# Adding the gMLP gate bias: from VectorE to sixteen one-row matmuls on TensorE

## The reference, cut to what matters

```python
def even_mixer(h, w_in, gmlp_w, gmlp_b, w_out, n_chunks):
    ...
    vn = (vf - jnp.mean(vf, axis=-1, keepdims=True)) * lax.rsqrt(jnp.var(vf, axis=-1, keepdims=True) + EPS)
    vn = vn.reshape(bsz, n_chunks, CHUNK, B_HEADS, B_DIM)
    z = jnp.einsum('hts,bnshc->bnthc', gmlp_w, vn) + gmlp_b.T[:, :, None]
    yb = u * z.reshape(bsz, t, B_HEADS, B_DIM)
    y = jnp.concatenate([ya.reshape(bsz, t, A_WIDTH), yb.reshape(bsz, t, B_WIDTH)], axis=-1)
    return y @ w_out
```

## Time and profile before

| what | value |
|---|---|
| median of three runs | 1981.9 us |
| the profiled execution's own time | 1978.92 us |
| its span (first to last instruction) | 1977.1 us |
| TensorE (PE) matmul busy | 1804.6 us, 91% |
| TensorE weight loads (PEld) busy | 1327.7 us, 67% |
| VectorE (DVE) busy | 837.1 us, 42% |
| ScalarE (ACT) busy | 660.7 us, 33% |
| chain that ended last, by engine | PE 69%, DMA 13%, DVE 10%, ACT 4%, SP's queue 3% |
| mean granted TensorE clock | 0.956 of full speed |
| time to landing of the broadcast bias load | 7.0 us |

### The profile page before, as it was taken

One profiled execution on the slowest core, in us unless ns is written; L12 is line 12 of the kernel. 1 busy time (PEld: TensorE's weight loads), 2 busy tenths in 40 slices (PEclk: granted clock), 3 DMA queues, 4 the chain that ended last, 5 costly groups with the idle time before them and its releaser, 6 DMA issues.

```text
span 1977.1 us, 28301 instructions
## 1 busy us (share of the span) xinstructions
PE 1804.6 (91%) x11584; PEld 1327.7 (67%) x11584; DVE 837.1 (42%) x1208; ACT 660.7 (33%) x829; POOL 3.4 (0%) x6
## 2 busy tenths in 40 slices
PE   4899899999999888988869999999989889998887
PEld 2667576787787678977857787766636777763433
DVE  2534522333233556467546975554203544420002
ACT  3232322221122355444336764444003434400001
POOL 0000000000000000000000000000000000000000
PEclk8899999999999899998968999999999999999997
DMA  8644166334532222221136989999999999999994
GB/s 320 252 160 149 45 243 226 136 96 141 200 92 80 64 84 66 64 79 40 65 126 216 369 298 363 409 409 409 408 409 404 357 360 380 389 409 409 409 409 167
DMA packets 161843, 479.96 MB, mean 243 GB/s; under 512 B 14976, under 2 KB 58160, under 8 KB 155568
## 3 DMA queue, kind: packets, MB, share of 16 engines
q1 hardware_dynamic: 161712, 478.14, 64.3%
HBM read 477.03 MB, written 1.05 MB: 242 GB/s over the span
## 4 chain that ended last, share of the span: by engine, by line
PE 69%; DMA 13%; DVE 10%; ACT 4%; SPq 3%; issue 2%; DVEq 0%; ACTq 0%
PE ps L603 15%; PE ps L604 14%; PE ps L605 14%; PE ps L1275 5%; DMA arena<-in_moe_up 5%; DMA raw<-in_moe_up 4%; PE ps L1346 3%; DMA arena<-in_moe_w 3%; SPq L553 2%; DVE w_lo L1769 2%; PE ps L617 2%; PE ps L1264 2%; PE ps L636 2%; PE ps L1096 1%; ACT w_hi L1415 1%
## 5 line engine op out<-in xcount | busy, mean ns | idle before, releaser
L1769 DVE TENSOR_TENSOR w_lo<-raw,w_hi 128x1024 fp32r<-128x1024 f32 x242 | 293.1, 1222 | 426.7 <-ACT w_hi L1415 424.2
L1415 ACT ACTIVATE w_hi<-raw 128x1024 fp32r<-128x1024 f32 x242 | 253.1, 1056 | 503.2 <-PE ps L605 399.3
L603 PE MATMUL ps<-h_hi,w_hi 128*128 128x512 f32 (+1 forms) x736 | 286.3, 389 | 27.3 <-DVE h_lo L1813 24.0
L604 PE MATMUL ps<-h_hi,w_lo 128*128 128x512 f32 (+1 forms) x736 | 278.2, 378 | 0.0
L605 PE MATMUL ps<-h_lo,w_hi 128*128 128x512 f32 (+1 forms) x736 | 277.4, 377 | 0.0
L1769 DVE TENSOR_TENSOR w_lo<-arena,w_hi 128x1024 fp32r<-128x1024 f32 x144 | 172.1, 1221 | 126.5 <-ACT w_hi L1415 123.6
L1415 ACT ACTIVATE w_hi<-arena 128x1024 fp32r<-128x1024 f32 x144 | 151.3, 1059 | 163.3 <-DMA arena<-in_moe_up 92.9
L603 PEld LDWEIGHTS ps<-h_hi,w_hi 128*128 128x128 f32 x736 | 142.4, 194 | 84.2 <-issue 54.6
L605 PEld LDWEIGHTS ps<-h_lo,w_hi 128*128 128x128 f32 x736 | 142.2, 193 | 25.8
L604 PEld LDWEIGHTS ps<-h_hi,w_lo 128*128 128x128 f32 x736 | 142.5, 194 | 22.5
L1275 PE MATMUL ps<-arena 128*64 128x256 f32 x1024 | 128.8, 387 | 10.0 <-DMA arena<-in_moe_up 8.4
(11 more groups left out here) (332 smaller groups left out, 2279.7 us busy)
## 6 DMA issues: line engine op xcount, KB each, us to landing
arena<-in_moe_up SPq DMA_DIRECT2D x256, 512.0 KB, 10.1
raw<-in_moe_up SPq DMA_DIRECT2D x192, 512.0 KB, 9.9
arena<-in_moe_w SPq DMA_DIRECT2D x128, 512.0 KB, 11.6
raw<-in_moe_w SPq DMA_DIRECT2D x96, 512.0 KB, 11.4
raw<-in_ffn_w SPq DMA_DIRECT2D x66, 512.0 KB, 5.1
arena<-in_w_ada SPq DMA_DIRECT2D x32, 1024.0 KB, 5.0
raw<-in_w_in_odd SPq DMA_DIRECT2D x40, 512.0 KB, 3.5
scratch<-in_w_ada SPq DMA_DIRECT2D x16, 1024.0 KB, 5.0
```

The costliest lines, as they stand in the source:

```text
L603: pe.matmul(dst, s_h, m_h, start=start, stop=False, **kw)
L604: pe.matmul(dst, s_l, m_h, start=False, stop=False, **kw)
L1415: act.activation(w_hi[:, o % R, :], src, ACT.Copy).then_inc(hi_done, 1)
L1769: dve.tensor_tensor(w_lo[:, o % R, :], src, w_hi[:, o % R, :].bitcast(F32), ALU.subtract).then_inc(lo_done, 1)
```

## The change

The bias is loaded as one row of 512 numbers into partition 32 of the arena. On TensorE every gate matmul is followed by a second fp32 matmul with a contraction over that single partition: a row of ones (`con`, partition 32) as the stationary tile and the head's 128 biases as the moving row. It accumulates into the same quarter bank. VectorE's addition goes, and its multiplication reads the bank of `ps` directly.

```diff
-        gate_bias = ar(GB_ROW, B_H * P)
+        gb_row = arena[32:33, GB_ROW:GB_ROW + B_H * P]
...
-            sp.dma_start(gate_bias, gmlp_b[0].rearrange("(a h) t -> a (h t)", a=1).broadcast_to([P, B_H * P])
-                         ).then_inc(mix_in, 16)
+            sp.dma_start(gb_row, gmlp_b[0].rearrange("(a h) t -> a (h t)", a=1)).then_inc(mix_in, 16)
...
             for h in range(B_H):
                 for t in range(TT):
                     m = pe.matmul(ps[:, 4 + h, t * P:(t + 1) * P], ar(M_V + t * BANK + h * P, P),
-                                  ar(M_GW + h * P, P), start=(t == 0), stop=(t == TT - 1), skip_group_check=True)
+                                  ar(M_GW + h * P, P), start=(t == 0), stop=False, skip_group_check=True)
+                    m = pe.matmul(ps[:, 4 + h, t * P:(t + 1) * P], con[32:33, C_ONE:C_ONE + P],
+                                  gb_row[:, h * P:(h + 1) * P], start=False, stop=(t == TT - 1),
+                                  skip_group_check=True)
                 m.then_inc(y_mm, 1)
...
-                tmp = ar(M_TMP + h % 2 * NT, NT)
-                b4 = gate_bias[:, h * P:(h + 1) * P].unsqueeze(1).broadcast_to([P, TT, P])
-                link(dve.tensor_tensor(tmp.rearrange("p (t c) -> p t c", t=TT),
-                                       ps[:, 4 + h, :].rearrange("p (t c) -> p t c", t=TT), b4, ALU.add))
-                dve.tensor_tensor(tmp, tmp, ar(M_U + h * NT, NT), ALU.mult).then_inc(y32_done, 1)
+                dve.tensor_tensor(ar(M_TMP + h % 2 * NT, NT), ps[:, 4 + h, :], ar(M_U + h * NT, NT),
+                                  ALU.mult).then_inc(y32_done, 1)
```

## The result

The changed kernel takes 1996.4 us in the median of four runs (1990.2 to 1998.9), the kernel before 1980.4. The medians are 16.0 us apart. The ratio, which is taken over the runs and not from the two medians, is 1.0074 (95% interval 1.0045 to 1.0102), which makes the kernel 14.7 us slower, from 8.9 to 20.2. The profiled execution took 1996.42 us, its span 1994.6.

The account below looks back on a forecast made before the run. The prediction took TensorE to bound the gate, with VectorE's addition hidden. Streaming 3.5, shape changes 6.4 and a clock fall 7 made 16.9 us on the median 1981.9, so 1998.8 us; the 8-in-10 range was 1985.5 to 2002.5.

Parts of the forecast that it names:

- VectorE's additions and the load at 0: Gate's four VectorE additions (0.68 us each) and bias load cut to 2 KB: both off the path, worth 0.
- channel tile 4: First output projection tile needing a gate head; last head ready 4.4 us ahead; TensorE waiting there would prove the forecast wrong.
- Term A: In the gate, sixteen one-row matmuls on TensorE stream at 0.218 us each, the single row saving nothing: 3.5 us.
- Term B: In the gate, 32 changes of TensorE's array shape at 0.20 us each: 6.4 us, bounds 0 and 7.0.
- Rival 2: In the gate, a shape change in rows alone costs nothing, only streaming stays: 3.5 us, 1985.4; chance 0.18.
- rival 3: In the gate, one-row matmuls stream hidden beside gate matmuls, so not slower: 1981.2, down to 1979; chance 0.06 with Rival 4.
- Term C: TensorE's clock falls to 0.50 some 3 us into the gate, lasting into the projection: 7 us, bounds 0 and 8.7.
- Rival 1: In the gate, shape changes cost as forecast but the clock holds: 9.9 us, 1991.8; chance 0.24.
- The sum: Streaming, shape changes and clock fall in gate and projection add 16.9 us, carried through to the program's end.
- Rival 4: After the gate, TensorE's delay is made up later and VectorE's relief is off any path; chance 0.06 with rival 3.

Follow-up runs that it names:

- two changes: Changed kernel with all sixteen gate matmuls first, then all sixteen one-row matmuls, so 2 changes of shape instead of 32; ratio 1.0010 to the kernel before.
- block, 32 rows: All gate matmuls, then sixteen bias matmuls holding and using 32 rows, against the changed kernel's alternating one-row matmuls; ratio 1.0011 to the kernel before.
- 64-row pairs: Changed kernel's alternating order and 32 changes of shape, but bias matmuls hold 64 rows and the bias is loaded broadcast; ratio 1.0037 to the kernel before.
- narrow: Changed kernel with 8 moving columns instead of 128 in each one-row matmul; from gate to next norm +15.44 us against the kernel before.
- eight: Changed kernel regrouped as four gate matmuls, then four one-row matmuls per head, so 8 changes of shape; ratio 1.0026 to the kernel before.
- sixteen: Changed kernel regrouped as two gate matmuls, then two one-row matmuls, eight times, so 16 changes of shape; ratio 1.0039 to the kernel before.

## Why the prediction was right

*VectorE's additions and the load at 0: right.* The stretch without them is that of before, 52.98 us, and keeping them beside the new matmuls changes nothing. No wait of TensorE on VectorE arose at channel tile 4. For the load only the kernel without a bias speaks, and only for the stretch behind the gate's start; what 0.7 us of transfers might move ahead of it can't be told from the scatter of that start (159.9 to 164.0 us over all profiles).

*Term A, streaming, 3.5 us: right.* 3.60 measured with 128 rows. One row saves nothing: the two-change gates take 7.43 us with one row as with 64.

*Term B, changes of shape, 6.4 us: right.* 6.17 measured, with 64 rows. That no row had a change in rows alone was the weak point; it costs what a change in columns does. The Trainium skill's rule ("TensorEngine Tiling (Array Packing)", Key Properties) that a change of mode drains the engine agrees with the 0.193 us. Rival 2, a free change in rows, is refuted, and with it rival 3.

*Term C, the clock, 7 us: right in that it falls, low in size, wrong in its cause.* It is 8.9 us in the stretch, just above my bound of 8.7. Of the parts, a pair at the lower clock takes 1.445 us (I had 1.41); the fall came 4.5 and 3.5 us in (I had 3); the projection then ran at half speed for 5.4 us (I had 3.2), and the clock didn't come back between. I took the cause from the gather of L1096 and wrote that for the rest of the time the array stands. The pauses are not enough: 32 of them with 64-row matmuls kept 1.00. What all eight profiles with a fall at this place have in common is matmuls that hold a strip of 32 rows, and two of them (two changes; block, 32 rows) have no pauses to speak of. Had the forecast gone by pauses alone, it would have put the kernel with 64-row pairs 9 us too high, and the one with two changes 1.7 us too low. Rival 1, a clock that holds, was a real case only for the wider shape.

A strip of 32 rows is neither the only way down nor a sure one. The gathers of L1096 hold all 128 rows and have no strip, and the clock falls at some of them. And the 32-row matmuls of L1144 in the kernel before, whose strips lie at two places of the array, kept 1.00 through a block of 2.9 us:

```profile
1745.40:1748.20 2.80, 2.80 (x18) 2.29 (x16) 0.00 (x0) 0.00 (x0) 0.00 (x0) 1.00 1.03 408
```

So what is shown is which shape brings the clock down here, not why. Whether the pauses add to it where strips and pauses come together is open too: the narrow matmuls stream hardly anything, and no run has them in another shape.

*The sum, 16.9 us: right within the interval, and in part by luck.* The stretch lost 18.7, 1.8 over the sum and nearly all of that in term C; the runs lost 14.7 by their ratio (8.9 to 20.2) and 16.0 by their medians. I had written that the sum carries through to the end, but a term that was too low and a loss that doesn't show in full at the end offset each other. The other kernels show the same leaning, by their ratios: two changes +5.6 in the stretch and +2.0 in the runs, eight +8.3 and +5.1, sixteen +12.8 and +7.7, 64-row pairs +9.8 and +7.3. Part of it can be named in single executions: at the first of the gathers of L1096 the clock fell in the profile of before, and the first expert matmul (L1275) comes 157.8 us after the routing's transposes start, against 154.1 in the profile of the changed kernel, where it didn't fall. Over all profiles it fell there in three of twelve with the same experts, in no order that goes with the edits. Whether that or something else makes the runs differ by less than the stretch stays open; no experiment was aimed at it. Rival 4, a delay that is made up later, is refuted as a whole, since most of it arrives; for a part of it the case is open.

Nothing here beats the kernel before: the addition on VectorE was hidden, and the cheapest of the ways tried to put it on TensorE costs 3.6 us of a stretch that TensorE bounds.

## What to carry to other kernels

Work that VectorE did in TensorE's shadow was free here; moved onto TensorE in a stretch where its busy time is 100%, it cost its full price, however small the arithmetic. A small contraction was not a small matmul here: it cost its moving columns, and alternated with full ones it cost two changes of shape each, 0.39 us here against 0.22 for the streaming. If such a matmul is needed, pad it to the full shape with zeros (+3.6 us here), or gather them into one block and don't leave it in a strip of 32 rows (+4.0 with 64, +5.5 with 32); and measure between two landmarks near the change when the runs scatter by more than it costs.

## What was not expected of the hardware

The granted clock went to 0.50 behind 3.7 us of one-row matmuls that streamed without a pause, and so it did when all 32 rows took part; 64 and 128 rows, with the same count and the same bias, left it at 1.00. At a shape change the open weight load and gap cost 0.19 us at the full clock and (1.445 - 4 x 0.213) / 2 = 0.30 at the lower one. And leaving out a small term of an early layer made the kernel 11% slower, since the experts that tokens choose, and with them the number of loop turns, hang on it: the expert matmul from `arena` (L1275, L1274 without the bias) has 1536 records without the bias and 1024 with it.
